# Routing two token tiles at a time in a mixture-of-experts kernel, with the first gathers of expert rows issued ahead of the barrier

## The chip, the cores and the metric

The kernel runs on one core of a Trainium2 chip. The metric is the device time of one execution in microseconds; lower is better.

## The reference

A two-block model in float32 on 1024 tokens of width 1024. The first block (window attention, a gated linear recurrence and an RWKV-like recurrence) is not touched by the change. The second block puts 16 meta tokens in front (1040 tokens) and has two layers, each a mixer (a short convolution, then latent attention), whose output projection is added to the hidden rows `h`, followed by a mixture of experts. The second layer keeps 1024 tokens. The part that matters here, for each layer:

```
h  = h + mixer(...) @ w_out                       # 1024 x 1024
hn = rmsnorm(h) * g
g_logits = hn @ w_grp                             # 8 groups
grp = argmax(g_logits)
e_in = the 8 expert logits (hn @ w_exp) of that group
the two largest e_in give the token's two experts, and the gates
each expert e: silu(x @ w_gate[e]) * (x @ w_up[e]) @ w_down[e]   # 64 experts, width 256
h  = h + sum of gate * expert output
```

## The kernel before

`moe` calls two functions for each layer. `back_and_route` makes `h`, normalises it and routes the tokens; `experts` runs the 64 experts on gathered rows. The words "routing stage" and "expert stage" below mean these two. Between them stands a barrier of all engines, since each is a block of its own.

**Tiles.** The tokens lie in tiles of 128 rows: nine in layer 0 (the ninth, with 16 rows, is done first as tile 0 and called the extra one; `EXTRA` is 1) and eight in layer 1. The others form pairs (x, y), four in each layer (`NP` is 4), and the output projection of a pair is one 2 x 2 block product with seven half-size products instead of eight, `p_1`, `p_2`, `p_6`, `p_5`, `p_7`, `p_4`, `p_3` in this order on TensorE. Each is 4 k-steps with a moving operand of 512 columns and appears in the trace as 8 instructions of line L1401 (`p_3` has line L1446). GpSimd makes the sums of token blocks (`token_sums`, L1308 to L1313), VectorE the sums of weight blocks once (`weight_sum`) and adds the products out of the accumulators into the rows of `h` (`e_1`, `c_11`, `u_1`, `u_2`, `c_22`, `c_21`, `c_12`, all L1592). `p_4` may start only when `u_2` has read its accumulator, `p_3` when `c_22` has, and the next pair's `p_1` when `c_21` has. The last half of tile y is complete with `c_12`, behind `p_3`.

**Routing of a tile.** It runs one iteration behind the products, in between them. ScalarE computes the squares and the root (`squares`) and stores the rows of `h` (`store`). TensorE transposes the rows (`turn`, two halves), ScalarE copies them out (`turned_out`), TensorE computes 72 logits (`logits`, L1469). VectorE normalises the rows (`scale`), and ScalarE stores them to the DRAM tensor `hn` (`store_scaled`, L1363). `pick` on VectorE finds the best group and the two best experts, in a chain of some twenty dependent instructions on 8 to 64 elements (L1629 to L1661), and leaves masks `chosen` and `both`. `ranks` on TensorE (L1479, L1480) counts, with a triangular matrix, how many earlier tokens chose the same expert, `place` on VectorE (L1666 to L1671) turns the count into one-hot rows `hot`, `table` on TensorE (L1487) puts the token numbers into their slots of a table of 64 experts x 64 places, and `gathered` on VectorE (L1678) adds the result to the table. Each of these works on one tile, and `ranks` of a tile waits for `gathered` of the one before. After the last tile four small instructions (L1751 to L1754) make the `queue` of row numbers.

**Experts.** They run in 32 pairs. The weights of a pair are 6 MB and go through a ring of three; those of the first three pairs are loaded within the routing stage (`early`, `late`: 9 MB of them when the last pair's products 5, 6 and 7 are done), but for 4 MB (`last_loads`), which SyncE issues when the first two gathers have landed. For each pair GpSimd gathers 128 rows from `hn` with an indirect DMA (`gather`, L2626), TensorE transposes them (L2451), multiplies (L2458, L2478), and GpSimd scatters the result. The first two gathers are GpSimd's first instructions in the expert stage. At the end of the routing stage GpSimd waits until all rows of `hn` are stored.

## Time and profile before

| what | us |
|---|---|
| median of three runs | 2905.14 (2904.2 to 2905.47) |
| the profiled execution | 2899.84, of it the span of the trace 2898.1 |
| routing stage, layer 0 and layer 1 (to the first transpose of an expert) | 997.6 to 1162.9, 2182.3 to 2341.2 |
| TensorE busy, over the span | 2532.5 (87%) |
| VectorE, ScalarE, GpSimd busy | 1097.3, 537.5, 227.3 |

Busy shares are means over stages with different limits. What a stage is worth has to be read from what is waited for in it, and at its end. All times in the trace are in microseconds from its start.

### The profile page before, as it was taken

The numbers are of one execution on the slowest core, as the hardware profiler recorded it, in microseconds if no ns is written. First come the engines' busy times: TensorE is split into PE (matmuls) and PEld (weight loads), VectorE is DVE, ScalarE is ACT, GpSimd is POOL, SyncE is SP. The second block draws the span as 40 slices with busy tenths as digits, with TensorE's granted clock in tenths as the row PEclk, the third lists the DMA queues.
The fourth block names the chain that finished last, engine by engine and source line by source line (L and its number), as shares of the span: only waits on it lengthen the run. The fifth ranks groups of instructions, "written<-read, shape, count | busy, mean of one in ns | idle before, by whom it ended". The sixth has DMA issues, their size and how long they took to land. (4 is left out here: it accounts for less than half of the span.)

```text
span 2898.1 us, 40495 instructions
## 1 busy us (share of the span) xinstructions
PE 2532.5 (87%) x16554; PEld 1632.2 (56%) x16554; DVE 1097.3 (38%) x2550; ACT 537.5 (19%) x1308; POOL 227.3 (8%) x278
## 2 busy tenths in 40 slices
PE   8999999998999997988788779999998978787882
PEld 3444569745888654555445545666664545554551
DVE  2324467556555555211101153544455531011014
ACT  0212355410000011111111132222221111111112
POOL 1000000000000210111111000000003011111110
PEclk9999999998999999999989989999999989999896
DMA  3101010131113144999999970000113489999997
GB/s 112 35 31 58 1 46 4 48 116 36 44 44 128 44 153 189 386 419 420 420 420 419 388 274 22 16 23 8 49 44 131 152 351 419 420 420 419 418 417 269
DMA packets 108028, 566.13 MB, mean 195 GB/s; under 512 B 21664, under 2 KB 21824, under 8 KB 56368
## 3 DMA queue, kind: packets, MB, share of 16 engines
q1 hardware_dynamic: 82656, 506.34, 43.5%
q0 software_dynamic: 20288, 39.32, 3.6%
q10 hardware_dynamic: 4896, 17.83, 1.5%
q8 instruction: 135, 2.21, 0.3%
q14 instruction: 53, 0.43, 0.0%
HBM read 529.06 MB, written 65.01 MB: 205 GB/s over the span
## 5 line engine op out<-in xcount | busy, mean ns | idle before, releaser
L2458 PE MATMUL ex__h_ps<-all__arena,ex__xT 128*64 128x256 f32 x3392 | 536.5, 422 | 176.1 <-DMA all__arena<-in_w_gate 112.0
L2458 PEld LDWEIGHTS ex__h_ps<-all__arena,ex__xT 128*64 128x64 f32 x3392 | 343.0, 153 | 351.9 <-issue 238.0
L2501 DVE COPY ex__ysb<-ex__y_ps 128x512 f32<-128x512 f32 x64 | 44.2, 691 | 646.9 <-PE ex__y_ps L2478 646.4
L290 PE MATMUL fr__acc<-X__xT,fr__w 128*128 128x512 f32 x640 | 280.1, 598 | 7.8 <-DMA X__xT<-in_xT 7.8
L290 PEld LDWEIGHTS fr__acc<-X__xT,fr__w 128*128 128x128 f32 x640 | 121.7, 191 | 163.8 <-issue 155.5
L2458 PE MATMUL ex__h_ps<-mo__wx,ex__xT 128*64 128x256 f32 x704 | 182.1, 418 | 0.0
L2478 PE MATMUL ex__y_ps<-b__w,ex__hT 128*64 128x512 f32 x672 | 152.2, 592 | 0.9 <-ACT ex__hT L2495 0.9
L1819 PE MATMUL cm__acc<-all__arena,cw__w 128*128 128x260 f32 x576 | 136.0, 386 | 2.6 <-PEq L84 2.6
L1819 PE MATMUL cm__acc<-all__arena,cm__sums 128*128 128x260 f32 x576 | 134.8, 384 | 0.0
L2626 POOL DMA_INDIRECT b__rows<-s_hn,mo__queue x64 | 64.9, 1014 | 869.7 <-PE ex__x_ps L2451 767.1
L1819 PEld LDWEIGHTS cm__acc<-all__arena,cw__w 128*128 128x128 f32 x576 | 110.4, 192 | 20.1 <-issue 3.0
L1819 PEld LDWEIGHTS cm__acc<-all__arena,cm__sums 128*128 128x128 f32 x576 | 110.1, 191 | 17.2
L2489 ACT ACTIVATE ex__sg<-ex__h_ps 128x256 f32<-128x256 f32 x64 | 24.5, 383 | 432.9 <-PE ex__h_ps L2458 432.9
L2458 PEld LDWEIGHTS ex__h_ps<-mo__wx,ex__xT 128*64 128x64 f32 x704 | 104.4, 151 | 0.0
L2492 DVE TENSOR_TENSOR ex__hs<-ex__sg,ex__h_ps 128x256 f32<-128x256 f32 x64 | 26.9, 421 | 186.6 <-PE ex__h_ps L2458 186.6
L2478 PEld LDWEIGHTS ex__y_ps<-b__w,ex__hT 128*64 128x64 f32 x672 | 54.0, 137 | 73.1 <-issue 67.5
L1401 PE MATMUL pb__acc<-b__w,all__arena 128*128 128x512 f32 x192 | 88.9, 608 | 4.3 <-POOL pb__eps L1303 4.3
L2483 ACT COPY ex__xT<-ex__x_ps 128x512 f32<-128x512 f32 x64 | 37.4, 585 | 292.0 <-PE ex__x_ps L2451 292.0
L1401 PE MATMUL pb__acc<-mo__wx,all__arena 128*128 128x512 f32 x192 | 87.3, 598 | 4.3 <-DVE b__rows L1592 2.5
L1064 PE MATMUL fo__acc<-all__arena 128*128 128x512 f32 x192 | 88.0, 609 | 1.9 <-PEq L84 1.9
L2185 PE MATMUL hd__o<-all__arena 128*128 128x128 f32 x704 | 85.6, 278 | 3.5 <-ACT all__arena L2242 3.5
L2451 PE MATMUL ex__x_ps<-mo__ident,b__rows 128*128 128x128 f32 x512 | 75.8, 292 | 12.8 <-DMA b__rows<-s_hn,mo__queue 12.8
(452 smaller groups left out, 3933.7 us busy)
## 6 DMA issues: line engine op xcount, KB each, us to landing
all__arena<-in_w_gate SPq DMA_DIRECT2D x106, 1024.0 KB, 26.6
all__arena<-in_w_up SPq DMA_DIRECT2D x106, 1024.0 KB, 26.2
b__w<-in_w_down SPq DMA_DIRECT2D x84, 1024.0 KB, 27.5
all__arena<-in_w_down SPq DMA_DIRECT2D x22, 1024.0 KB, 22.5
mo__wx<-in_w_gate SPq DMA_DIRECT2D x22, 1024.0 KB, 28.6
mo__wx<-in_w_up SPq DMA_DIRECT2D x22, 1024.0 KB, 29.6
mo__wx<-in_w_down SPq DMA_DIRECT2D x22, 1024.0 KB, 29.9
all__arena<-s_ys SPq DMA_DIRECT2D x16, 1024.0 KB, 8.2
```

Of the source, the lines that this page charges most:

```text
L290: last = mm(acc[:, b, c], wbuf[:, b, k], xT[:, k, 512 * c:512 * c + 512], start=(k == 0), stop=(k == KT - 1))
L1064: last = nc.tensor.matmul(acc[:, t % 2, c], proj[:, G_T + k, P * t:P * t + P], wo[k][:, 512 * c:512 * c + 512], start=(k == 0), stop=(k == ...
L1401: last = mm(acc[:, bank], weight[:, k], moving[:, k], start=(first and k == 0), stop=(last_here and k == HK - 1), skip_group_check=not first)
L1819: last = nc.tensor.matmul(bank(u, x), weight(k), moving(k, c), start=(k == 0), stop=(k == HK - 1))
L2185: last = mm(o_ps[:, h, 0:P], vv[:, s, h], pT[:, h, a], start=(a == 0), stop=(a == len(tiles) - 1))
L2451: last = nc.tensor.transpose(x_ps[:, k // 4, P * (k % 4):P * (k % 4) + P], xe[:, b, k::KT], ident[:])
L2458: last = nc.tensor.matmul(h_ps[half, c, DE * b:DE * b + DE], xT[:, b, k, half], slots[n][:, c, k], start=(k == 0), stop=(k == KT - 1))
L2478: last = nc.tensor.matmul(y_ps[half, c], hT[:, b, k, half], slots[n][:, k, 512 * c:512 * c + 512], start=(k == 0), stop=(k == 1))
L2483: return nc.scalar.copy(xT[:, b, 0:4].rearrange("p k q -> p (k q)"), x_ps[:, 0])
L2492: return nc.vector.tensor_tensor(hs[:, b], sg[:, b], h_ps[:, 1, DE * b:DE * b + DE], ALU.mult)
L2501: return nc.vector.tensor_copy(ysb[:, b, 512:], y_ps[:, 1])
L2626: g.indirect_dma_start(xe[:, p % 2], None, hn_dram[:, :], bass.IndirectOffsetOnAxis(ap=queue[:, 0, p:p + 1], axis=0), bounds_check=T - 1, ...
```

## The change

It does these things, in both layers.

- `pick`, `ranks`, `place`, `table` and `gathered` work on a group: a pair of tiles, or the extra tile by itself. Small tensors get a dimension for the tile in the pair (`lane`). The compare with a pointer operand and two operations in `first_max` becomes two plain instructions, so that a pair can be done in one. The gate differences `gdiff` and `ed` move behind the mask.
- In the order of TensorE both tiles' logits stand ahead of `p_5`, `ranks` of the pair ahead of `p_4`, and `table` of the pair between `p_4` and `p_3`. `ranks` waits for the one-hot rows of the group before (it writes other columns than `table`), not for the table's read-out. On VectorE `pick` of the pair stands ahead of `u_2`, for the extra tile too.
- The last iteration is ordered anew: table, logits and transposes are set between halves and quarters of `p_4` and `p_3`.
- TensorE waits for GpSimd's constants behind `p_2(0)`, not ahead of `p_1(0)`.
- The last tile's normalised rows are made by GpSimd (times `g`) and ScalarE (times the root's reciprocal) instead of VectorE's `scale`. On ScalarE the last tile's `store_scaled` stands behind this, and those of the last pair behind both tiles' copies and squares.
- ScalarE ends the routing stage with a Silu on one column.
- The gathers of expert pairs 0 and 1 are issued by GpSimd at the end of the routing stage, after all rows of `hn` are stored and the queue is ready, and are gone from the expert stage.

The core of the diff:

```diff
@@ GpSimd, end of back_and_route
                 g.memset(xe[:], 0.0).then_inc(xe_clear, 1)
+                j = TT - 1
+                pool.wait_ge(hn_stored[j % 2], 16 * (j // 2))
+                for c, part_of in enumerate((low, high)):
+                    half_ready(pool, j, c)
+                    tt(hn[:, j % 2, part_of], rows[slot_of(j)][:, part_of], gb[:, part_of], ALU.mult).then_inc(gained, 1)
                 pool.wait_ge(xe_clear, 1)
                 for b in range(2):
                     pool.wait_ge(hn_stored[b], 16 * ((TT + 1 - b) // 2))
+                pool.wait_ge(queue_done, 1)
+                for p in range(2):
+                    g.indirect_dma_start(xe[:, p], None, D["hn"][0:T, :],
+                                         bass.IndirectOffsetOnAxis(ap=queue[:, 0, p:p + 1], axis=0),
+                                         bounds_check=T - 1, oob_is_err=False).then_inc(x_loaded[p], 16)
@@ ScalarE, last pair
-                    squares(x)
                     if n == NP - 1:
                         turned_out(x)
+                        squares(x)
                         store(x)
+                        turned_out(y)
+                        squares(y)
                         store_scaled(x)
-                        squares(y)
-                        turned_out(y)
                         store(y)
+                        act.wait_ge(gained, 2)
+                        act.wait_ge(rs_last, 1)
+                        nc.scalar.activation(hn[:, y % 2], hn[:, y % 2], ACT.Copy, scale=rs[:, lane(y):lane(y) + 1]
+                                             ).then_inc(scaled, 1)
                         store_scaled(y)
...
+                nc.scalar.activation(warm[:], eps[:], ACT.Silu)
@@ TensorE
+                def ranks(q):
+                    pe.wait_ge(picked, q + 1)
+                    if q:
+                        pe.wait_ge(hot_done, q)
+                    else:
                         pe.wait_ge(const_done, CONSTS)
+                    for j in groups[q]:
+                        earlier = [both[:, lane(i)] for i in groups[q] if i < j] + [before[:, q]]
+                        mm(rank_of[:, lane(j)], up[:], both[:, lane(j)], start=True, stop=False)
+                        for i, counts in enumerate(earlier):
+                            last = mm(rank_of[:, lane(j)], ones[:], counts, start=False, stop=(i == len(earlier) - 1))
+                    last.then_inc(ranked, 1)
...
-                pe.wait_ge(const_done, 5)
...
                 x, y = X[NP - 1], Y[NP - 1]
+                p_4(NP - 1, range(0, HK // 2))
+                table(LAST - 1)
+                p_4(NP - 1, range(HK // 2, HK))
                 turn(x, 1)
                 p_3(NP - 1, range(0, HK // 2))
                 turn(x, 0)
-                table(x - 2)
-                p_3(NP - 1, range(HK // 2, HK))
-                ranks(x - 1)
-                logits(x)
+                p_3(NP - 1, range(HK // 2, HK - 1))
+                logits(x, (0,))
                 turn(y, 0)
+                p_3(NP - 1, range(HK - 1, HK))
+                logits(x, (1,))
                 turn(y, 1)
-                table(x - 1)
                 logits(y)
-                ranks(x)
-                table(x)
-                ranks(y)
-                table(y)
+                ranks(LAST)
+                table(LAST)
@@ VectorE
+                def first_max(values, best, hot_at, s, shape):
                     v(red(best, values, AX.X, ALU.max))
-                    v(stt(out=cand[:], in0=values, scalar=best, in1=pri[:], op0=ALU.is_equal, op1=ALU.mult))
-                    v(red(m8[:], cand[:], AX.X, ALU.max))
+                    v(tt(cand[:, s], values, best.unsqueeze(2).to_broadcast(shape), ALU.is_equal))
+                    v(tt(cand[:, s], cand[:, s], pri[:].unsqueeze(1).to_broadcast(shape), ALU.mult))
+                    v(red(m8[:, s], cand[:, s], AX.X, ALU.max))
+                    v(tt(hot_at, cand[:, s], m8[:, s].unsqueeze(2).to_broadcast(shape), ALU.is_equal))
...
                 if EXTRA:
                     scale(0)
+                    pick(0)
                 u_2(0)
                 c_22(0)
                 if EXTRA:
-                    pick(0)
+                    place(0)
                 c_21(0)
                 c_12(0)
+                if EXTRA:
+                    gathered(0)
                 for n in range(1, NP):
-                    if x >= 1:
-                        place(x - 1)
                     e_1(n)
-                    if x >= 1:
-                        gathered(x - 1)
                     scale(x)
                     c_11(n)
                     scale(y)
                     u_1(n)
-                    pick(x)
+                    pick(q)
                     u_2(n)
                     c_22(n)
-                    pick(y)
+                    place(q)
                     c_21(n)
-                    place(x)
                     if n == NP - 1:
+                        gathered(q)
                         scale(X[n])
                     c_12(n)
-                    gathered(x)
+                    if n < NP - 1:
+                        gathered(q)
-                place(x - 1)
-                scale(y)
-                gathered(x - 1)
-                pick(x)
-                pick(y)
-                place(x)
-                gathered(x)
-                place(y)
-                gathered(y)
+                pick(LAST)
+                place(LAST)
+                gathered(LAST)
@@ experts, GpSimd
-                for b in range(2):
-                    gather(b)
```

In `pick(LAST)` the reciprocal of the last tile's root is computed behind the product with the expert logits (`root_of_last`), and signals ScalarE.

## Rows read from the trace of the kernel before

**Rows 1.** The page, slices of the span: GB/s moved by DMA in each fortieth

```profile
GB/s 112 35 31 58 1 46 4 48 116 36 44 44 128 44 153 189 386 419 420 420 420 419 388 274 22 16 23 8 49 44 131 152 351 419 420 420 419 418 417 269
```

**Rows 2.** The chain that ended last: start, length, what

```profile
2337.68 3.45 DMA b__rows<-s_hn,mo__queue
```

**Rows 3.** TensorE's waits, 995 to 1165 us: in total, times, longest

```profile
PE pb__rk_ps L1487 <- DVEq L1674: 9.4, 5, 5.6
PE ex__x_ps L2451 <- DMA b__rows<-s_hn,mo__queue: 6.5, 1, 6.5
PE pb__tp L1502 <- POOL pb__eps L1303: 5.1, 1, 5.1
...
PE pb__rk_ps L1479 <- DVEq L1679: 2.8, 4, 1.0
```

**Rows 4.** Windows: busy time by engine, granted clock, DMA share and GB/s

```profile
1033.54:1067.80 34.26, 31.64 (x130) 17.31 (x130) 20.75 (x64) 6.26 (x14) 7.81 (x7) 1.00 0.32 123
1067.80:1101.06 33.26, 31.65 (x131) 17.32 (x130) 19.44 (x63) 5.04 (x11) 2.12 (x2) 1.00 0.27 95
...
1150.00:1155.00 5.00, 1.73 (x12) 1.44 (x12) 2.58 (x10) 0.00 (x0) 0.00 (x0) 0.50 0.76 320
...
2212.46:2246.16 33.70, 31.07 (x121) 17.01 (x120) 19.53 (x59) 6.01 (x12) 7.94 (x7) 1.00 0.48 187
```

**Rows 5.** Timeline of TensorE, layer 0: start, length, what, idle before

```profile
1125.12 3.70 PE L1401 MATMUL pb__acc<-mo__wx,all__arena 128*128 128x512 f32 x8 [0.45 <-DVE pb__ho L1592]
...
1139.80 1.98 PE L1469 MATMUL pb__lg_ps<-b__wr,pb__hnT 128*128 128x72 f32 x16
1144.97 0.69 PE L1479 MATMUL pb__rk_ps<-pb__both,pb__up 128*128 128x64 f32 x2 [3.19 <-DVEq L1660]
...
1151.65 0.65 PE L1487 MATMUL pb__rk_ps<-mo__chosen,pb__hot 128*64 128x32 f32 x8 [5.56 <-DVEq L1674]
...
1162.92 1.97 PE L2451 MATMUL ex__x_ps<-mo__ident,b__rows 128*128 128x128 f32 x8 [6.49 <-DMA b__rows<-s_hn,mo__queue]
```

**Rows 6.** Timeline of VectorE, layer 0

```profile
1025.43 1.49 DVE L1592 TENSOR_TENSOR b__rows<-pb__acc,b__rows 128x512 f32<-128x512 f32 x2 [5.80 <-PE pb__acc L1401]
...
1140.17 0.17 DVE L1629 TENSOR_REDUCE pb__gm<-pb__lg_ps 128x1 f32<-128x8 f32 x1
...
1156.87 0.18 DVE L1754 TENSOR_SCALAR mo__queue<-mo__queue 128x32 int32<-128x32 int32 x1
```

**Rows 7.** Timeline of GpSimd and TensorE at layer 1's entry

```profile
2182.35 0.20 POOL L1297 MEMSET mo__ident<- 128x128 f32 x1 [385.91 <-POOLq L84]
...
2185.11 9.24 PE L1401 MATMUL pb__acc<-b__w,all__arena 128*128 128x512 f32 x16 [4.28 <-POOL pb__eps L1303]
```

**Rows 8.** VectorE's groups, 1140 to 1158 us: busy, mean ns, idle before

```profile
L1671 DVE TENSOR_SCALAR pb__hot<-mo__row,mo__rk,mo__ids 128x64 f32<-128x64 f32 x4 | 1.1, 311 | 0.1
L1631 DVE TENSOR_REDUCE pb__m<-pb__cand 128x1 f32<-128x8 f32 x6 | 1.0, 162 | 0.2
...
L1666 DVE TENSOR_TENSOR pb__sel<-mo__chosen,pb__rk_ps 128x128 f32<-128x128 f32 x2 | 0.6, 288 | 1.4 <-PE pb__rk_ps L1480 1.3
...
L1659 DVE TENSOR_TENSOR pb__both<-mo__chosen 128x64 f32<-128x64 f32 x2 | 0.5, 225 | 0.1
```

**Rows 9.** Timelines of ScalarE, GpSimd and SyncE around layer 0's barrier

```profile
1139.88 0.50 ACTq L1363 DMA_DIRECT2D s_hn<-pb__hn  x1
...
1159.34 1.16 POOL L2626 DMA_INDIRECT b__rows<-s_hn,mo__queue  x1 [45.78 <-POOLq L84]
...
1164.43 0.33 SPq L2370 DMA_DIRECT2D all__arena<-in_w_gate  x1
```

**Rows 10.** Line L1363, stores of normalised rows: the whole trace

```profile
DMA to landing us min/median/max: 2.6/5.0/13.5
```

**Rows 11.** DMA queues, 1151 to 1152 us: packets, MB, engines' share

```profile
q10 hardware_dynamic: 36, 0.11, 27.3%
```

**Rows 12.** Line L1310, a token sum: ns min, median, max

```profile
L1310 POOL TENSOR_TENSOR all__arena<-all__arena x8: 1262/1265/3211, 999.8 to 2244.5; 128x512 f32<-128x512 f32 x8
```

More of the change, by code:

```diff
@@ L1434, in p_7, with p_4 @@
                     product_of(n, A, s_3(n), t_3, False, True)
[L1436 to L1439 removed]
+                def p_4(n, ks):
+                    if ks[0] == 0:
+                        pe.wait_ge(summed, 7 * n + U2)
+                        pe.wait_ge(t_made, 4)
+                    for k in ks:
+                        last = mm(acc[:, A], a22(n)[:, k], t_4[:, k], start=False, stop=(k == HK - 1),
+                                  skip_group_check=True)
+                    if ks[-1] == HK - 1:
+                        last.then_inc(product, 1)
                 def p_3(n, ks):
@@ L1472, in ranks @@
-                def ranks(j):
-                    pe.wait_ge(picked, j + 1)
-                    if j >= 1:
-                        pe.wait_ge(tbl_out, j)
+                    if group_of(j):
+                        pe.wait_ge(lg_out, group_of(j))
+                    for n in halves:
+                        pe.wait_ge(evac, 2 * j + 1 + n)
+                        c = halves_of(j)[n]
+                        for i, k in enumerate(range(HK * c, HK * c + HK)):
+                            last = mm(lg_ps[:, lane(j), 0:LG], hnT[:, j % 2, k], wr[:, k], start=(n == 0 and i == 0),
+                                      stop=(n == 1 and i == HK - 1))
+                        last.then_inc(lg_done, 1)
@@ new lines, in place @@
+                def place(q):
+                    tiles, s, t = groups[q], lanes(q), places(q)
+                    dve.wait_ge(ranked, q + 1)
+                    v(tt(sel[:, s], chosen[:, t], rank_of[:, s].unsqueeze(2).to_broadcast([P, len(tiles), 2, EXPERTS]),
+                         ALU.mult))
+                    v(red(rk[:, t], sel[:, s], AX.X, ALU.add))
+                    if q:
+                        dve.wait_ge(tabled, q)
+                    for j in tiles:
+                        for c in range(2):
+                            at_j = place_of[j]
+                            v.hold(ts(hot[:, lane(j), c], row[:], rk[:, at_j, c:c + 1], ids[:, at_j, c:c + 1],
+                                      ALU.is_equal, ALU.mult))
```

204 lines of the change are left out of this document (103 added, 101 removed).

## The prediction

> **What bounds the kernel now.** I read the page's slices of DMA rate first. Each expert stage (about 1166 to 1650 and 2345 to 2831 us) stands at 417 to 420 GB/s, the highest rate of the kernel [rows 1]: it moves the expert weights and can't be shortened by anything in this change. But it starts only when TensorE gets its first gathered rows, and the chain that ended last runs through exactly that gather at 2337.68 [rows 2]. So a microsecond taken off ahead of the gather should arrive whole at the end, twice, once a layer. Ahead of it lies the routing stage, 997 to 1163 us in layer 0, 2182 to 2341 in layer 1.
>
> The second view is TensorE's waits in that stage [rows 3]: 9.4 us for one-hot rows (five waits, one of them 5.6), 2.8 us in four waits of `ranks` for the table's read-out, 6.5 us for the gather, 5.1 us at the entry for GpSimd's constants. Third, windows cut at the start of `p_1` [rows 4]: a middle iteration lasts 34.26, 33.26 and 33.70 us, of which TensorE works about 31.6 (31.1 in layer 1's first); the rest is those small waits. Fourth, the end in time order: the last logits run from 1139.80 [rows 5], VectorE then routes two tiles one after the other, 1140.17 to 1157.05 [rows 6], and the first transpose of an expert starts at 1162.92 [rows 5]. That stretch of 21 us has almost no product in it and is what the change rewrites. Layer 1's tail is the same, 1178.4 us later.
>
> **Entry.** `p_1(0)` no longer waits for GpSimd's five constants. GpSimd starts at 2182.35, TensorE at 2185.11 [rows 7], 2.8 us later; in layer 0 the corresponding gap is 0.9 us, from GpSimd's first instruction at 997.6 to TensorE's at 998.55, the end of its 5.1 us wait. The next thing that can stop TensorE is `p_6`: it needs the second token sum, which GpSimd has 4.6 us after 2185.03, at 2189.65, while TensorE gets there about 2191 even then. Nothing is late. I take −0.9 and −2.9; bounds 0 and −4.4, the latter if TensorE also escapes the lower of its two clocks, at which it starts now: its first sixteen product instructions last 9.24 us [rows 7], where eight at the full clock take 3.7 [rows 5].
>
> **First iteration of layer 0.** `pick(0)` moves ahead of `u_2`. Today `u_2` starts at 1025.43, as soon as P7 is there [rows 6]. The logits of tile 0 end near 1021.8; one `pick` now takes 4.8 us to its mask (1140.17 to 1144.97, where `ranks` starts [rows 5, 6]), and the counts and two gate differences behind it bring it to 5.7, hence 1027.5. `u_2` is 2.1 us later, and `p_4`, which waits for it, too: +2.1. Bounds 0 and +3.
>
> **Middle iterations.** A pair's `pick` has 15 small steps for 12 (the masked comparison is split) and processes 128 elements where it had 64. A tiny step is 162 ns and about 40 to the next; 64 more elements cost 0.288 − 0.225 = 0.06 us [rows 8]. From today's 4.8: +0.6 for three steps, +0.3 for five wider ones, −0.4 for steps with a pointer that become plain ones, −0.5 for the gate differences and a signal moved behind: 4.9 us to the mask for both tiles, against 2 × 4.8. Counts and four gate differences add 1.6: 6.5. What covers it is `p_5` and `p_7`, 2 × 3.44 = 6.9 us: with both logits now ahead of `p_5`, `pick` starts 0.2 after the second. So `u_2` isn't delayed, by a margin of 0.4 us. The five rank matmuls (0.8 us) fall into the wait that `p_4` has for `u_2` anyway (0.45 today, behind 0.55 of ranks). `place` for two tiles is done 10.7 us after the logits, `p_4` at 11.3: the table (as many matmuls as two before) doesn't wait. So the waits before the table and before the second `ranks` vanish (0.5 + 0.66 in the second iteration, 1.51 + 0.66 in the first), and 0.5 to 0.6 of the second `ranks` and hand-overs: 31.5 us. Against [rows 4]: −2.8 and −1.8 in layer 0, −2.2 and −1.8 in layer 1.
>
> **The last iteration and the tail, in layer 0's times.** `p_4` starts 0.36 earlier than now (1125.12 [rows 5]), since `table` behind `p_1` is gone: 1124.76. Its second half waits for `place` of the pair, about 1.0 us, and 0.7 of table follows. P4 is complete at 1129.9 (now 1128.7), P3, with half the logits and three half tiles' transposes between, at 1135.6 (1135.1). `scale(x)` ends at 1136.5 and only then comes `c_12`, so `turn(y, 1)` runs at 1137.3 and the last logits end at 1139.4; now they end at 1141.6, because two ranks and a table stood ahead. From 1139.6: mask 5.3 (4.9, and the reciprocal and its signal inside); five ranks 2.6 (two take 1.1 at the lower clock, 0.69 and 0.64 [rows 5], each more 0.49); `place` 2.1 (two wider steps 0.9, four one-hots of 0.31, partly overlapped [rows 8], and a signal); table 1.2 (0.65 [rows 5] for half as many); read-out and four queue steps 1.2. The queue is ready at 1152.0, not 1157.05: −5.0.
>
> Now the gather. It needs the queue and all normalised rows in memory. The last store is issued at 1139.88 today [rows 9], and stores of these rows take up to 13.5 us [rows 10], since the stage's last 9 MB of weights are streaming: ACT's queue still moves in 1151 to 1152, with 27% [rows 11], and DMA is busy 0.76 of 1150 to 1155 [rows 4], so to about 1154. The change issues the x tile's rows at 1139.8 (now 1134.6) and the y tile's at about 1142.4, after GpSimd's product, VectorE's reciprocal (1141.3) and ACT's scaling (1.0). 1.57 MB at 0.11 to 0.15 MB per us would last beyond the stream; but with the weights done they get the full rate, and the bytes in all are unchanged. So they land between 1152.3 and 1154.5; I take 1153.2. That, not the queue, then releases the gather: 1.2 of the 5.0 is lost. Behind it: 0.9 to GpSimd's first issue, two issues, 1.16 [rows 9] and 1.02, with 0.3 between, then the barrier, 1.1 (VectorE ends at 1157.42, GpSimd is released at 1158.5): TensorE starts 4.5 after, 1157.8, when the first rows (3.5 after their issue) are just there. Now 1162.92. The last weights, which SyncE holds until both gathers have landed, go at 1159.1, not 1164.43 [rows 9]. −5.3; bounds −6.4 (queue decides) and −3.9 (1154.5).
>
> The Silu table load (1.3 us today, beside the first 5.2 us of gate products) moves to where ACT is idle: nothing, and it costs nothing if it stayed.
>
> GpSimd's new product of the last tile may meet VectorE. A GpSimd product of this size takes 1262 ns alone and up to 3211 beside VectorE [rows 12]. Its second half starts with `c_12`, 1137.3, and ends at 1138.6, a microsecond ahead of `pick`. Drawn out to 3.2 us it would end at 1140.5, still before the reciprocal of 1141.3 for which the scaling also waits, but inside `pick`, whose steps would be late. The Trainium skill (SBUF — State Buffer, "Reading the diagram") says that a VectorE instruction with two SBUF inputs and a GpSimd one that reads SBUF exclude each other for a whole instruction. By that rule a meeting would cost one GpSimd product per layer, which would make the sum about 2.5 us smaller; the trace's two durations agree with it, and the times say they don't meet.
>
> **Sum.** Layer 0: −0.9 + 2.1 − 4.6 − 5.3 = −8.7. Layer 1: −2.9 − 4.0 − 5.3 = −12.2. Together −20.9. The profiled execution took 2899.84 (span 2898.1 and 1.7 around it), so the next should take 2878.9; the median, 5.3 above it, goes from 2905.14 to 2884.2.
>
> **Rivals.**
> - *The rows land late.* The late stores of the last tile queue behind each other until after the weights, and both tails gain only 3 to 3.9: −18, 2887; with 2 us more, −14, 2891. For it: a store took 13.5 us in this traffic [rows 10]. Against: bytes are conserved. 0.22.
> - *VectorE blocks the products.* Each us e by which the pair's mask is longer than 4.9 costs, past the margin of 0.4, one us in each of four middle iterations and two per tail: 8e − 4.6. At e = 1, −17.5; at e = 3.2, a mask after 8.1 us, it is even; if two tiles cost twice one (9.6), +13 to +14 and 2919. This is the slower side: 0.05. For it: the compares read with broadcast operands along two axes, which no row shows with four dimensions. Against: [rows 8] show time by elements only. A small e (0.5 to 2.5), 2888 to 2899: 0.07.
> - *The head start isn't passed on*: the weight stream waits for something else, or the barrier with GpSimd last in it is dearer, and the loops' gain alone is eaten by `pick(0)`. Within 0.2%: 0.04. Against: the whole stage is at one rate [rows 1].
> - *GpSimd and VectorE meet*, as above: 2886.7, 0.05.
>
> Forecast as summed: 0.57. 0.2% (5.8 us) is about what a measurement can tell from no change. Faster 0.91, same 0.04, slower 0.05. The range: the best bounds of entry, first iteration and tails give −20.9 − 1.5 − 2.1 − 2.2 = −26.7; the other end takes in late rows and a mask 1 us longer, −12: 2878 to 2893.
>
> **What would show it.** Right: middle iterations of 31.3 to 31.8 us; a wait of 2 us ahead of layer 0's first `p_4`; queue ready 12.6 us after the last logits; both gathers issued before the barrier, first transpose some 18 us after the last logits' end (21.3 now); the whole expert stage as long as now. Wrong: a wait before each `p_4` (VectorE), over 2.5 us between queue and gather (rows), an expert stage longer by what the routing stage lost.

## The result, and the profile after

| what | before | after |
|---|---|---|
| median, us | 2905.04 (2904.20 to 2905.47, four runs) | 2886.86 (2885.75 to 2888.38, four runs) |
| ratio after to before, 95% interval | | 0.994, 0.9924 to 0.9956 |
| the profiled execution, us | 2899.84, span 2898.1 | 2885.75, span 2883.7 |

The kernel is 18.2 us (0.6%) faster by the medians and 14.4 us by the spans of the two traces. The forecast was 20.9. The rest is read from traces, and there the whole program isn't the best scale: in the thirteen traces of this study, whose kernels share all code ahead of layer 0's routing stage, that stage starts anywhere between 994.97 and 1000.70 us. So stages are measured from their own first instruction, which is GpSimd's first clear of `ident`. In the changed kernel that is at 998.31 and 2178.51, in the one before at 997.63 and 2182.35.

**Middle iterations.** The windows of the changed kernel from one `p_1` to the next, two of layer 0 and the first whole one of layer 1 (columns as in [rows 4]):

```profile
1037.49:1069.01 31.52, 31.52 (x132) 17.71 (x131) 15.72 (x45) 5.04 (x10) 5.05 (x4) 1.00 0.36 134
1069.01:1100.52 31.51, 31.51 (x132) 17.70 (x130) 15.70 (x45) 5.04 (x10) 5.03 (x4) 1.00 0.29 101
2205.66:2237.17 31.51, 31.51 (x131) 17.70 (x130) 15.60 (x44) 5.33 (x11) 5.04 (x4) 1.00 0.50 201
```

TensorE's busy time, the second number, is now the whole window: it waits for nothing. VectorE, the fourth, fell from 20.75 and 19.44 [rows 4] to 15.7, in 45 instructions for 64 and 63. Nor does the pair's `pick` hold up the sums. VectorE begins it at 1053.27, has the mask at 1058.15 and the rest at 1059.66, and then itself waits 0.52 us for `p_7`:

```profile
1060.18 1.49 DVE L1631 TENSOR_TENSOR pb__ho<-pb__acc,pb__ho 128x512 f32<-128x512 f32 x2 [0.52 <-PE pb__acc L1427]
```

**First iteration of layer 0.** TensorE's timeline of the changed kernel (start, length, what, idle before it):

```profile
1023.36 3.65 PE L1427 MATMUL pb__acc<-b__w,all__arena 128*128 128x512 f32 x8
1028.23 0.43 PE L1513 MATMUL pb__rk_ps<-pb__both,pb__up 128*128 128x64 f32 x2 [1.23 <-DVEq L1707]
...
1029.96 3.70 PE L1467 MATMUL pb__acc<-mo__wx,all__arena 128*128 128x512 f32 x8 [1.07 <-DVE b__rows L1631]
```

The number in brackets is TensorE's wait: first for the mask of tile 0, then for `u_2`. These waits are the price of `pick(0)` ahead of `u_2`: from the start of `p_7` to that of `p_4` it takes 6.60 us, before 4.42.

**Entry of layer 1.** GpSimd and TensorE; [rows 7] is the same place before:

```profile
2178.51 0.20 POOL L1307 MEMSET mo__ident<- 128x128 f32 x1 [385.67 <-POOLq L84]
...
2178.81 8.74 PE L1427 MATMUL pb__acc<-b__w,all__arena 128*128 128x512 f32 x16 [1.98 <-PEq L84]
```

TensorE starts 0.30 after GpSimd, not 2.76, and its two first products last 8.74 instead of 9.24.

**The end of layer 0's routing stage.** ScalarE's queue, VectorE, GpSimd, TensorE and SyncE in order of time; [rows 9] and [rows 5] have the places before:

```profile
1138.99 0.40 ACTq L1371 DMA_DIRECT2D s_h<-pb__ho  x1
...
1141.55 0.33 ACTq L1383 DMA_DIRECT2D s_hn<-pb__hn  x1
...
1150.97 0.18 DVE L1808 TENSOR_SCALAR mo__queue<-mo__queue 128x32 int32<-128x32 int32 x1
...
1154.35 1.16 POOL L1351 DMA_INDIRECT b__rows<-s_hn,mo__queue  x1 [16.85 <-DMA s_hn<-pb__hn]
1155.81 1.02 POOL L1351 DMA_INDIRECT b__rows<-s_hn,mo__queue  x1 [0.30 <-issue]
1160.33 0.14 POOL L2689 IOTA ex__steps_i<- 128x16 int32 x1 [3.50 <-POOLq L84]
...
1160.36 1.94 PE L2505 MATMUL ex__x_ps<-mo__ident,b__rows 128*128 128x128 f32 x8 [8.94 <-PEq L84]
...
1160.38 0.33 SPq L2424 DMA_DIRECT2D all__arena<-in_w_gate  x1
```

Three things are to be seen. The queue is ready at 1151.15. GpSimd's release names the store of normalised rows, not the queue, and its first gather comes 3.2 us behind the queue. And after its last issue (ended 1156.83) all engines start the next stage together only at 1160.3. The view of this line over the whole trace says how long after their issue the gathers' rows land:

```profile
DMA to landing us min/median/max: 3.4/3.5/3.9
```

The second gather of layer 0 has 3.5: 1155.81 and 3.5 is 1159.3, and the stage starts 1.0 later. In layer 1 the second gather is issued at 2324.37, lands 3.9 later, and the stage starts at 2329.32, again 1.0 to 1.1 later.

Where the 14.4 us come from, in pieces of each routing stage (the last piece ends where SyncE issues the last weights):

| piece | layer 0, before, after | layer 1, before, after | forecast |
|---|---|---|---|
| start to the second `p_1` | 35.91, 39.18: +3.27 | 30.11, 27.15: −2.96 | +1.2, −2.9 |
| two middle iterations | 67.52, 63.03: −4.49 | 66.97, 63.03: −3.94 | −4.6, −4.0 |
| the fourth `p_1` to the last weights | 63.37, 59.86: −3.51 | 63.92, 60.68: −3.24 | −5.3, −5.3 |
| sum | −4.73 | −10.14 | −8.7, −12.2 |

The sum is −14.9; the stages around them make up +0.5.

### The profile page after: what moved, and what is told of

Read it like the earlier page. It is cut to its first block and busy times, and to the rows that moved or that the text cites. A ratio compares the mean times of both kernels' runs of the same rounds, so it can differ in the third digit from the quotient of the medians.

```text
span 2883.7 us, 40366 instructions
## 1 busy us (share of the span) xinstructions
PE 2532.8 (88%) x16578; PEld 1634.7 (57%) x16578; DVE 1064.7 (37%) x2404; ACT 540.4 (19%) x1312; POOL 230.5 (8%) x282
## 5 line engine op out<-in xcount | busy, mean ns | idle before, releaser
L2505 PEld LDWEIGHTS ex__x_ps<-mo__ident,b__rows 128*128 128x128 f32 x512 | 63.3, 195 | 42.9 <-issue 42.9
```

Source lines behind the costliest of these rows:

```text
L2505: last = nc.tensor.transpose(x_ps[:, k // 4, P * (k % 4):P * (k % 4) + P], xe[:, b, k::KT], ident[:])
```

## The experiments

Each kernel was timed five times or more, beside the kernel before. That kernel's own executions lie between 2898.3 and 2907.4 us and its medians between 2901.6 and 2905.0, so rows are compared by their ratios and not by their medians, and differences of 1 to 3 us can't be read from either. The conclusions rest on the traces, one of each kernel and two of the changed one, and on two places above all: W, SyncE's issue of the last weights, and T, the first transpose of expert rows, both counted from GpSimd's first instruction of the routing stage.

| kernel | median, us | ratio to before, 95% interval | T, W in layer 0 | T, W in layer 1 |
|---|---|---|---|---|
| before | 2901.6 to 2905.0 | | 165.29, 166.80 | 158.83, 161.00 |
| after | 2886.86 | 0.994 (0.9924 to 0.9956) | 162.05, 162.07 | 150.84, 150.86 |
| gathers_back | 2886.58 | 0.9952 (0.9938 to 0.9966) | 160.94, 162.52 | 148.39, 150.06 |
| pad | 2889.15 | 0.9953 (0.994 to 0.9967) | 162.69, 162.72 | 150.56, 150.59 |
| stores_first | 2883.86 | 0.9942 (0.9928 to 0.9956) | 160.56, 160.59 | 147.79, 147.81 |
| pick0_back | 2885.78 | 0.9946 (0.9932 to 0.996) | 158.96, 158.99 | 150.53, 150.55 |
| weights_sooner | 2893.75 | 0.9967 (0.9955 to 0.9979) | 165.94, 157.73 | 153.58, 145.69 |
| before_gathers | 2902.10 | 0.9995 (0.9986 to 1.0004) | 166.34, 166.37 | 160.33, 160.36 |
| const_back | 2888.36 | 0.9951 (0.9937 to 0.9964) | 161.98, 162.00 | 153.44, 153.46 |
| scale_back | 2887.92 | 0.9945 (0.9931 to 0.9958) | 162.62, 162.65 | 150.43, 150.46 |
| first_only | 2885.68 | 0.9937 (0.9924 to 0.9951) | 160.71, 160.67 | 148.81, 148.77 |
| best | 2878.85 | 0.9919 (0.9905 to 0.9932) | 155.46, 155.42 | 146.47, 146.42 |
| after_again | 2888.15 | 0.9947 (0.9933 to 0.9961) | 162.67, 162.70 | 149.98, 150.01 |

Four rows have W where nothing should move it (after, after_again, pad, scale_back): 162.07 to 162.72 in layer 0 and 150.01 to 150.86 in layer 1. A difference in W below 0.7 and 0.9 us isn't told from chance.

The table shows by itself what the rest of the program hangs on. What lies behind the two Ws (from W of layer 0 to the start of layer 1's routing stage, and from W of layer 1 to the end of the span) is 1572.7 us before, 1572.5 after, and 1571.3 to 1574.5 in all others but weights_sooner, whatever T does.

**gathers_back.**

```diff
@@ end of the routing stage, GpSimd
-                pool.wait_ge(queue_done, 1)
-                for p in range(2):
-                    g.indirect_dma_start(xe[:, p], ...).then_inc(x_loaded[p], 16)
@@ head of the expert stage, GpSimd
+                for b in range(2):
+                    gather(b)
```

> The two gathers go back to the head of the expert stage, the rest of the change stays. Theory A (a block's closing barrier also waits until the rows that GpSimd's own gathers ask for have landed, about 1.0 us beyond the landing): in layer 0 GpSimd is released at about 1153.4 as now, a barrier of 1.1 us follows, the gathers are issued at 1155.4 and 1156.9, the first transpose starts at about 1159.0 (now 1160.36) and the last weights go at about 1160.5 (now 1160.38). So whole time 2885.5 to 2887.5, the same as with the gathers ahead (2886.9). Rival, the forecast's step (ahead of a barrier of 1.1 us the gathers save about 1.4 us of weight stream a layer): 2889 to 2890. Both say that pairing alone holds nearly all of the gain.

Without the move the kernel is the same to within the spread: it is 15.0 us below the kernel before, where the changed kernel was 18.2 below in one comparison and 15.6 in another, and W is +0.45 in layer 0 and −0.8 in layer 1. GpSimd's timeline of gathers_back:

```profile
1155.03 1.16 POOL L2675 DMA_INDIRECT b__rows<-s_hn,mo__queue  x1 [17.92 <-POOLq L84]
1156.49 1.03 POOL L2675 DMA_INDIRECT b__rows<-s_hn,mo__queue  x1 [0.30 <-issue]
1157.53 0.16 POOL L2686 IOTA ex__steps_i<- 128x16 int32 x1
```

The barrier lies ahead of the gathers here. T is 1.1 and 2.4 us earlier than with the gathers ahead, since the first rows may be used as soon as they land, and nothing comes of it. The forecast's rival value (1.4 us of W a layer) isn't there. So the move of the gathers is worth nothing that can be measured, and the gain is that of the rest: the pairing, with its order, and the constants' wait.

**before_gathers**, the same question from the other side:

```diff
@@ the kernel before, end of back_and_route, GpSimd
+                pool.wait_ge(queue_done, 1)
+                for p in range(2):
+                    g.indirect_dma_start(xe[:, p], ...).then_inc(x_loaded[p], 16)
@@ the kernel before, experts, GpSimd
-                for b in range(2):
-                    gather(b)
```

> The kernel before, with one part of the change alone: the first two gathers issued in the routing stage, behind the queue. Theory A (the barrier waits for their landing and 1.0 us more): last weights 166.6 us after GpSimd's first instruction in layer 0 (166.80 before) and 160.3 in layer 1 (161.00), so 0.9 us faster in all, no change that can be measured; the first transposes at 166.6 instead of 165.3. Rival, the forecast's step (a barrier of 1.1 us with the landing behind it): last weights some 1.4 to 2 us earlier in each layer, 3 to 4 us in all, 0.10 to 0.14% faster.

W is 166.37 and 160.36 (−0.43 and −0.64, too little to tell from nothing), T is 1.05 and 1.5 us later, the ratio 0.9995. The rival's 1.4 to 2 us of W a layer isn't there, which agrees with theory A.

**pad** tells a wait that runs from the gather's issue from one that runs from GpSimd's last instruction:

```diff
@@ behind the two gathers in the routing stage, GpSimd
+                g.memset(hn[:], 0.0)
```

> After the two gathers in the routing stage GpSimd clears a scratch tile that nobody reads any more (128x2048, 1.8 us by the clearing of the row buffers), and so ends at about 1158.7 instead of 1156.8. Theory A (the barrier waits for the landing of GpSimd's gathers, some 3.5 us after the second issue, and then 1.0): the pad is covered, the expert stage starts where it did, 3.5 us after the second gather's issue has ended (1160.3), and the whole is 2886 to 2888. Rival B (a barrier after a software DMA always takes 3.5 us from GpSimd's last instruction): the stage starts 1.8 us later in each layer, whole 2889.5 to 2891.

GpSimd's timeline of pad:

```profile
1158.79 1.02 POOL L1351 DMA_INDIRECT b__rows<-s_hn,mo__queue  x1 [0.30 <-issue]
1159.82 1.82 POOL L1354 MEMSET pb__hn<- 128x2048 f32 x1
1163.37 0.14 POOL L2690 IOTA ex__steps_i<- 128x16 int32 x1 [1.73 <-POOLq L84]
```

The wait behind GpSimd's last instruction fell from 3.50 to 1.73 us: the pad is covered whole. From the second issue to the next stage it is 4.58 us (4.52 in the changed kernel), in layer 1 5.03 (4.95). Rival B is out by the trace. The median doesn't help: 2889.15 is above the 2886 to 2888 of theory A and 0.35 below the rival's range.

pad by itself leaves open whether the barrier waits for the landing or for a fixed time from the issue. Two views of all ten traces with a gather ahead of the barrier settle it. First, the landing isn't always the same, and the stage follows it. In the eight kernels with both gathers ahead, the next stage starts 4.47 us after the second issue where the rows landed 3.4 us after it, 4.52 to 4.58 for 3.5, 4.63 to 4.67 for 3.6, 4.77 for 3.7, 4.90 to 4.97 for 3.9 and 5.03 for 4.0. Second, the barrier has records of its own. GpSimd ends the stage with a DRAIN (its queue's line, L1279, duration in ns, then its start), here in the changed kernel, pad, best and gathers_back:

```profile
L1279 POOLq DRAIN  x1: 4777/4777/4777, 1154.6 to 1154.6; - x1
L1279 POOLq DRAIN  x1: 4800/4800/4800, 1157.6 to 1157.6; - x1
L1279 POOLq DRAIN  x1: 3826/3826/3826, 1148.8 to 1148.8; - x1
L1279 POOLq DRAIN  x1: 38/38/38, 1153.3 to 1153.3; - x1
```

With a gather ahead it lasts 3.8 to 5.2 us, in both layers of all ten traces, and ends within 0.2 us of the landing of the last such gather (1154.6 and 4.8 is 1159.4; the landing is at 1159.3). In the three kernels without one it lasts 34 to 38 ns. So it is this DRAIN that waits, and for the rows. The 1.0 us behind it is the rest of the barrier, with the clearing of semaphores in it (0.24 us from 1159.8), which the kernel before has too: 1.1 us from VectorE's end at 1157.42 to 1158.5.

**stores_first.**

```diff
@@ ScalarE, last pair
                         squares(x)
-                        store(x)
                         turned_out(y)
                         squares(y)
                         store_scaled(x)
-                        store(y)
                         ...
                         store_scaled(y)
+                        store(x)
+                        store(y)
```

> ScalarE stores the normalised rows of the last two tiles ahead of the plain rows of both (the two plain stores are issued last). Theory S (the gathers are released by the landing of the last normalised rows, 2.3 us behind the queue, since two more stores lie in front of them): these rows land up to 1.2 us earlier, GpSimd's first issue moves from 1154.35 to 1152.1 to 1153.3, and the plain rows' landing takes over as the barrier's condition without being later than the gathers' landing: whole 2882.5 to 2885.5. Rival: the transfers of the weights that share the same DMA engines end at 1152.6 whatever the order, and every store ends with them: no change, 2886 to 2888.

Timelines of ScalarE and GpSimd in stores_first:

```profile
1142.45 0.33 ACTq L1383 DMA_DIRECT2D s_hn<-pb__hn  x1
1142.87 1.09 ACTq L1371 DMA_DIRECT2D s_h<-pb__ho  x2
...
1153.09 1.16 POOL L1351 DMA_INDIRECT b__rows<-s_hn,mo__queue  x1 [14.69 <-DVEq L1809]
```

The releaser is now VectorE's signal behind the queue, which was ready at 1152.06, 1.03 us ahead of the gather; it was the store. The last rows' store lands 9.5 us after its issue at 1142.45, at 1152.0; in the changed kernel 11.9 us after 1141.55, at 1153.4. W is 1.5 us earlier in layer 0 and 3.05 in layer 1 than in the changed kernel (2.1 and 2.2 against after_again). The theory holds, with the gather 1.6 us earlier in layer 0, counted in the stage (expected were 1.0 to 2.2), and the plain stores don't take over: ScalarE, which waits for them, leaves the stage at 1155.8, and GpSimd's DRAIN ends at 1158.3.

**pick0_back.**

```diff
@@ VectorE
                     scale(0)
-                    pick(0)
                 u_2(0)
                 c_22(0)
-                    place(0)
+                    pick(0)
                 c_21(0)
                 c_12(0)
-                    gathered(0)
```

With it `ranks(0)` on TensorE goes from behind `p_7(0)` to behind `p_3(0)`, `table(0)` from behind `p_4(0)` to behind `p_1(1)`, and `place(0)` and `gathered(0)` on VectorE around `e_1(1)`.

> The last tile's routing (layer 0 alone has a ninth tile) goes back behind the sum of the second quarter, as in the kernel before: its picking, its ranks behind the last product of the first iteration, its table in the second iteration. Theory: its place ahead of that sum costs TensorE the 2.2 us that the first iteration grew by from the seventh to the fourth product (6.60 against 4.42 us), so this kernel is 1.8 to 2.4 us faster, 2884.5 to 2885.1, with the second iteration at 31.5 to 32.0 us. Rival: the wait only moves on, since ranks and table of that tile then lie in the second iteration (which was 34.26 us before the change): up to 1.5 us given back there, 2886 to 2887.

W is 3.1 us earlier in layer 0 than in the changed kernel (3.7 against after_again), more than the 2.2 expected. The medians don't show it: pick0_back is 15.8 us below the kernel before, where the changed kernel was 15.6 and 18.2 below. The second `p_1` starts 35.32 us into the stage (39.18 and, in after_again, 39.79), the second iteration is 32.08 for 31.52. What goes beyond the stall of 2.2 is TensorE's clock. TensorE's timeline of the same place in the changed kernel's second trace (after_again), and its windows there (granted clock is the third number from the right):

```profile
1028.60 0.43 PE L1513 MATMUL pb__rk_ps<-pb__both,pb__up 128*128 128x64 f32 x2 [1.24 <-DVEq L1707]
...
1030.33 5.40 PE L1467 MATMUL pb__acc<-mo__wx,all__arena 128*128 128x512 f32 x8 [1.07 <-DVE b__rows L1631]
```

```profile
1028.40:1030.40 2.00, 0.73 (x5) 0.59 (x5) 1.49 (x6) 0.00 (x0) 0.00 (x0) 1.00 1.01 426
1030.40:1033.40 3.00, 3.00 (x5) 1.26 (x6) 1.69 (x5) 0.00 (x0) 0.00 (x0) 0.61 0.28 117
```

The second window has a mean of 0.61: behind the two waits, some 0.7 us into `p_4`, the clock falls from 2.4 to 1.2 GHz, and `p_4` takes 5.40 us for 3.70. Five more traces with `pick(0)` ahead have the 5.40: gathers_back, pad, stores_first, weights_sooner and scale_back. Three have 3.70: the changed kernel's first, const_back and first_only. But there the low clock with which the stage begins lasts longer (0.50 until 1004.3 in the changed kernel's first trace, 5.5 us from its first product; until 1003.3 in after_again, 3.0 us from it), and the extra rows' first products take 6.43, 6.14 and 6.54 us instead of 4.96 to 5.33. So either way it is 39.2 to 39.8 us to the second `p_1`. The two traces with `pick(0)` back, pick0_back and best, have neither: 4.91 and 5.26, 3.70, and 35.3 and 35.7 us. The slow first products run long before `pick(0)`, so that its place causes them isn't shown; what is shown is that the fall inside `p_4` came in six of nine traces with `pick(0)` ahead and in none of the four without (the kernel before, before_gathers, pick0_back and best). Why one or the other happens no run tells.

**const_back.**

```diff
@@ TensorE, ahead of extra_products and p_1(0)
+                pe.wait_ge(const_done, 5)
```

> TensorE again waits for GpSimd's five first constants ahead of the routing stage's first product. Theory: layer 1 gives back the 2.5 us by which the first product then starts later (2.76 against 0.30 us after GpSimd's first instruction) plus the later step of the clock, 2.5 to 3.0 in all at the second iteration's start (27.15 now); layer 0 gives back 0.4 (0.92 against 0.52). Whole 2.9 to 3.4 us slower than the changed kernel. Rival (weight sums, token sums or the extra rows' sum end last in the first iteration): layer 1 less than 1 us slower.

TensorE's timeline of const_back at layer 1's entry:

```profile
2179.39 9.20 PE L1427 MATMUL pb__acc<-b__w,all__arena 128*128 128x512 f32 x16 [4.43 <-POOL pb__eps L1313]
```

The second `p_1` is at 30.06 for 27.15, W at 153.46 for 150.86: 2.9 and 2.6 us. Nothing else is late in that iteration; the rival is out. In layer 0 nothing shows (39.30 us to the second `p_1`). Its median, 2888.36, is 1.5 above the changed kernel's first and 0.2 above its second, where 2.9 to 3.4 were expected; the spread allows either.

**scale_back.** VectorE scales the last tile's rows within the last pick, and GpSimd's two products and ScalarE's scaling are gone.

```diff
@@ VectorE, pick of the last group
-                        root_of_last()
+                        scale(TT - 1)
```

> The last tile's rows are scaled by VectorE alone, in one operation of 1.1 to 1.3 us within the last pair's picking, where the reciprocal of the root now stands; GpSimd's two products and ScalarE's scaling fall away. Theory: the queue is ready 1.1 to 1.3 us later (154.0 to 154.4 us after GpSimd's first instruction in layer 0 by the 152.84 of now, 142.0 in layer 1 by 140.8), but the last rows' store is issued earlier or at the same time and still lands behind the queue, so the gathers' release and the whole move by less than 0.5 us a layer: the split over three engines is covered by the stores. Rival (the queue or its barrier decides): 1.1 to 1.3 us a layer, 2.2 to 2.6 us slower.

VectorE's scaling takes 1.28 us, the queue is ready at 154.33 and 141.83 (152.84 and 140.80 with the three engines), and W is 162.65 and 150.46, within the two traces of the changed kernel. GpSimd is still released by the store. As it stands the split over three engines is covered by the stores; with the stores first, where the queue releases, it would count.

**weights_sooner**, on gathers_back:

```diff
@@ SyncE, head of the expert stage
-                for b in range(2):
-                    sp.wait_ge(x_loaded[b], 16)
+                sp.wait_ge(asked, 1)
@@ GpSimd, behind gather(1)
+                pool.sem_inc(asked, 1)
```

> Both gathers at the head of the expert stage, as in the kernel gathers_back, and SyncE issues the last four weight transfers as soon as GpSimd has asked for both gathers, no longer once they have landed. Theory W (the expert stage hangs on the moment at which the weight stream goes on, and on nothing that TensorE does with the first rows): the last weights go at 159.9 us after GpSimd's first instruction of the routing stage in layer 0 (162.52 in gathers_back) and at 147.4 (150.06) in layer 1, the first transposes up to 1.5 us later than in gathers_back, since rows and weights share the DMA engines, and the whole is 3 to 5.2 us faster than gathers_back (2881.4 to 2883.6 by its median). Rival P (the first pair's rows and TensorE's half clock set the pace of the ring): no gain or up to 2 us slower.

The expectation failed: 3 to 5.2 us faster than gathers_back was expected, and against the kernel before it gains 9.9 us where gathers_back gains 15.0, with a span 8.8 us longer than that of gathers_back. Its premise failed too. GpSimd, SyncE and TensorE of weights_sooner:

```profile
1157.17 1.16 POOL L2675 DMA_INDIRECT b__rows<-s_hn,mo__queue  x1 [17.92 <-POOLq L84]
1158.64 1.03 POOL L2675 DMA_INDIRECT b__rows<-s_hn,mo__queue  x1 [0.30 <-issue]
...
1157.51 0.33 SPq L2419 DMA_DIRECT2D all__arena<-in_w_gate  x1
...
1165.72 1.97 PE L2501 MATMUL ex__x_ps<-mo__ident,b__rows 128*128 128x128 f32 x8 [12.54 <-DMA b__rows<-s_hn,mo__queue]
...
1174.79 0.81 SPq L2419 DMA_DIRECT2D all__arena<-in_w_gate  x2
```

The signal came 0.3 us after the first gather had begun to be issued, before the second. So the weights went first, the gathers' rows landed 8.5 and 10.2 us after their issue for 3.5, and T is 5 us late. The ring's next weights wait for the first pair's gate products, and were issued at 1174.79, 175.0 into the stage; in gathers_back at 169.06. From 1170 to 1175 the DMA engines are mostly idle:

```profile
1170.00:1175.00 5.00, 5.00 (x32) 2.85 (x30) 0.00 (x0) 0.20 (x1) 0.00 (x0) 0.62 0.22 66
```

0.22 is their busy share; it is 1.01 in the changed kernel from 1165 on. Rival P has the mechanism right and its size too small (it allowed 2 us). Behind W stands a second limit, T, by an estimate some 3 us away (in gathers_back the ring's next issue comes 6.5 us after W, and the last weights, 4.2 MB at 0.42 MB per us, keep the DMA engines busy for 10). The rest of the program takes 1588.4 us instead of 1572.5. The Trainium skill (Perfetto Trace Analysis, "DMA Instruction — SWDGE (GPSIMD)") says that the profiled end of such an instruction is that of the descriptors' making, not of the transfer; the trace agrees: in the changed kernel the record of the second gather lasts 1.02 us, and its rows land 3.5 us after its start.

**first_only**, from what the last two taught: T and W together, both behind one landing.

```diff
@@ end of the routing stage, GpSimd
-                for p in range(2):
+                for p in range(1):
                     g.indirect_dma_start(xe[:, p], ...).then_inc(x_loaded[p], 16)
@@ head of the expert stage: GpSimd, SyncE
+                gather(1)
...
-                for b in range(2):
-                    sp.wait_ge(x_loaded[b], 16)
+                sp.wait_ge(x_loaded[0], 16)
```

> The changed kernel with the first gather alone ahead of the barrier, the second at the head of the expert stage, and SyncE's last weights behind the landing of the first gather instead of both. By theory A (the barrier ends 4.5 to 4.9 us after the last gather's issue ahead of it) the expert stage starts 1.4 us earlier in each layer, and the weights and the first transposes with it: last weights 160.6 us after GpSimd's first instruction in layer 0 (162.07 now) and 149.4 in layer 1 (150.86). The second rows, needed only some 10 us into the stage, share the DMA engines with the weights and still are there in time. Whole 2.9 us faster than the changed kernel. Rival P (as when the weights went before the gathers had landed): the rows that share with the weights come over 5 us late, and the second pair or the ring's next weights wait: same or up to 3 us slower.

W is 160.67 and 148.77: 1.4 and 2.1 us earlier (2.0 and 1.2 against after_again). The second rows land 9.8 and 9.2 us after their issue, beside the weights, and TensorE doesn't wait for them (in layer 0 they land at 1170.8 and are transposed from 1171.81). By its median it is 1.2 us below the changed kernel and 2.5 below after_again, for the 2.9 expected. Of the 3.5 us of W, 0.6 to 2 may be given back in the expert stages (1574.5 us behind the Ws for 1573.9 and 1572.5).

**best** and **after_again.** best is first_only with the edits of stores_first and pick0_back; after_again is the changed kernel once more.

> first_only together with the two edits that helped alone: the normalised rows' stores ahead of the plain ones, and the last tile's routing back behind the second quarter's sum. By the sum of the parts, last weights at 155.3 to 156.2 us after GpSimd's first instruction in layer 0 (162.07 in the changed kernel; 158.99 with the routing of the last tile back, 1.5 less for the stores, 1.4 less for the single gather) and at 146.2 to 146.6 in layer 1 (150.86; 147.81 with the stores first, 1.4 less for the single gather): 10 to 11 us faster than the changed kernel, 2875 to 2878. Rival (all bytes, plain rows too, must be in memory before the stage ends, so in layer 0 the barrier passes from the gather to the plain stores): layer 0 at 157 to 158, 8 to 9 us in all.

> The changed kernel once more, on the chip of these two, as the base of their comparison: whole 2884 to 2889. All but the clock's steps and the stages upstream should repeat: iterations of 31.5 us, last weights at 162.0 to 162.7 us after GpSimd's first instruction in layer 0 and 150.5 to 150.9 in layer 1. If the low clock in the first product of layer 0 (6.4 us for the extra rows' products, 5.0 to 5.3 in others with the same code) was one execution's chance, it is 5.0 to 5.3 here, and the fourth product of the first iteration takes 5.4 us instead of 3.7, as it did in all of those.

GpSimd and SyncE of best in layer 0:

```profile
1149.02 1.16 POOL L1351 DMA_INDIRECT b__rows<-s_hn,mo__queue  x1 [14.69 <-DVEq L1814]
1154.19 1.02 POOL L2684 DMA_INDIRECT b__rows<-s_hn,mo__queue  x1 [4.01 <-POOLq L84]
...
1153.50 0.33 SPq L2429 DMA_DIRECT2D all__arena<-in_w_gate  x1
```

W is 155.42 and 146.42, where the sum of the parts had it; the plain stores don't take over, though ScalarE leaves the stage only at 1151.8, 0.8 us before GpSimd's DRAIN ends. The median, 2878.85, is 0.85 above the expected 2875 to 2878. It is 9.3 us below after_again on the same chip, and 24.9 (0.8%, interval 0.9905 to 0.9932) below the kernel before, where the change as made gives 15.6 there. after_again repeats all but the place of the low clock, which came as expected: 5.33 and 5.40.

## Why the prediction was right, and where it was off

2884.2 was forecast, 2886.86 came, inside the range and on the forecast side, with 2.7 us of 20.9 missing by the medians. The loops and the entry gave it their part by the mechanism that was forecast; one of the change's parts, the gathers' move, gave nothing, and the total stayed inside since the range's slow end had allowed for late rows. By the traces 6.0 are missing (−14.9 for −20.9). The profiled execution of before lay 5.2 us below its median, that of after 1.1 below, so part of the closeness is luck; in later comparisons the change gave 15.6 (after_again) and, without the gathers' move, 15.0 us.

- **Middle iterations**: right. 31.5 us forecast, 31.51 and 31.52 measured in both layers. VectorE doesn't block the products, with 0.5 us to spare for the 0.4 forecast. In the last pair, with the reciprocal inside, the mask took 5.30 us from `pick`'s start at 1138.69 to `ranks` at 1143.99, as forecast, and the queue was ready 12.5 us after the last logits' end (1138.65), for 12.6. No run undoes the pairing by itself: its 4.5 and 3.9 us are read from the windows before and after.
- **Entry**: right in layer 1, −2.96 for −2.9 and put back by const_back (+2.9). In layer 0 the start moved by 0.40 for 0.9, and a longer low clock took it back (6.43 us for the first products, before 5.10; 5.33 in after_again).
- **First iteration of layer 0**: the mechanism was right and mis-sized. The stall was 2.2 us for 2.1. With the entry it is +3.3 in the first trace and +3.9 in the second, for +1.2. The term left out the clock. In the second trace 1.7 of the excess are `p_4`'s, behind the stall; in the first 1.3 are those of the first products, ahead of it, which the stall can't have caused. pick0_back gets 3.1 to 3.7 of W back.
- **The last iteration**: the queue came 5.36 us earlier, counted from the fourth `p_1`, for 5.0.
- **The rows' landing**: mis-sized. Forecast 1.2 us behind the queue, measured about 2.3 (3.2 and, in layer 1, 3.6 from the queue to the gather, over the 2.5 us that the prediction had named as the sign of late rows). The rival "the rows land late" thus names a part of what happened, and its number, 2887, is nearer than the forecast's. Counted from the fourth `p_1`, the gather came 0.8 us later than forecast in layer 0 and 1.2 in layer 1, although the queue was 0.3 early. stores_first takes it away.
- **The step "then the barrier, 1.1"**: this one failed. Behind gathers issued ahead of it the barrier lasts until they have landed and 1.0 us more, 3.5 and 3.95 us after the last issue's end, most of it in GpSimd's DRAIN. That made W another 1.0 and 1.4 us late, and TensorE's start 2.4 (6.9 us after the release for 4.5). So the gathers' move brought nothing, as gathers_back and before_gathers show. The prediction had "the barrier with GpSimd last in it is dearer" as half of a rival at 0.04, too little, though right that it alone wouldn't undo the gain. One of its signs of being right thus failed: the first transpose came 21.7 us after the last logits' end, not 18, and that is no sooner than before (21.3).
- **The whole expert stage as long as now**: right, 1572.5 us behind the two Ws for 1572.7. The stage hangs on the weight stream as the prediction took it, but first_only and weights_sooner show TensorE's first pair close behind it.
- **Silu's table load**: 1.28 us at 1141.90, in ScalarE's idle time. The one that opened the expert stage (1165.54 before) is gone; two later ones, around the gates, stay as before (1187.22 and 1188.90). No run undoes it, so that it costs nothing is only what the trace suggests. **GpSimd's product** took 1.27 us at 1136.23, alone: it doesn't meet VectorE.
- **Two sums of the prediction** don't come out as written: today's 4.8 with its four corrections is 4.8 and not 4.9, and its formula 8e − 4.6 gives +12 us, 2917, for a mask of 9.6 us and not 2919. Nothing in the forecast hangs on either.

## What to carry to other kernels

A transfer that GpSimd issues ahead of a stage's closing barrier to save its latency can be waited for by that barrier, here in GpSimd's DRAIN; ask what the barrier waits for before counting the latency as hidden, and put ahead of it only the transfer that the next stage needs first. When a step at the end of a stage gets faster, find what is now last, here two plain stores in front of the one that matters, and reorder it too. A routine put ahead of the sum that the next product waits for costs its length once and, in six of nine traces here, the granted clock a second time, so off the loop's steady state (one iteration, no cover) it belongs behind.

## What the runs showed that was not expected

- In all ten traces with a gather ahead of the barrier, the next stage starts 4.4 to 5.0 us after the issue of the last such gather, with 1.8 us of other GpSimd work behind it or none. That is 1.0 to 1.1 us after its landing (3.4 to 4.0 us), up to which GpSimd's DRAIN lasts: 3.8 to 5.2 us, against 34 to 38 ns without such a gather.
- A signal that follows both gathers in GpSimd's order let SyncE issue weights 0.3 us after the gather's first record began, ahead of the second gather's record: it doesn't say that the gathers have been handed over.
- Two waits of 1.24 and 1.07 us close together on TensorE were followed in six of nine traces by a granted clock of 1.2 GHz for some 3 us, and in the three others not, where the first products, at the low clock, had taken 0.8 to 1.6 us longer.
- A gather of 0.5 MB lands 3.5 us after its issue on idle DMA engines, and 8.5 to 10.2 us after it beside 4.2 MB of weights.
